# ScalarE's copy of a weight slot in two halves, each with its own signal to GpSimd

## Time and profile before

| | us |
|---|---|
| median of 3 runs | 2040.75 |
| lowest and highest | 2040.41, 2041.22 |
| the profiled execution's own time | 2041.43 |
| its span, first to last instruction | 2039.6 |
| TensorE busy | 1947.3 |
| VectorE busy | 1171.2 |
| GpSimd busy | 996.3 |
| ScalarE busy | 746.4 |

### The profile page before, as it was taken

How to read it: one execution, slowest core, us unless ns; L and a number is a source line. 1 busy time by engine, 2 the same in 40 slices (tenths; PEclk the granted TensorE clock), 3 DMA queues, 4 the chain that set the end, 5 groups by cost and what they waited for, 6 DMA issues and landing times.

```text
span 2039.6 us, 24806 instructions
## 1 busy us (share of the span) xinstructions
PE 1947.3 (95%) x9028; PEld 1609.5 (79%) x9028; DVE 1171.2 (57%) x2101; ACT 746.4 (37%) x1096; POOL 996.3 (49%) x1271
## 2 busy tenths in 40 slices
PE   7999989999899899999999999998999999999997
PEld 5778768787778778788888888787887888888886
DVE  6996659977676657655332324666576553232335
ACT  5334434335324445333322313344454223232230
POOL 5334253342543344656646456633344656464643
PEclk9999999999999999999999999999999999999998
DMA  4221122221222222222322222221122222222221
GB/s 173 89 75 67 56 83 104 76 73 63 73 83 71 75 83 76 90 103 83 109 93 94 103 98 88 86 101 62 63 83 104 94 92 99 87 104 103 83 103 63
DMA packets 28058, 178.92 MB, mean 88 GB/s; under 512 B 3872, under 2 KB 4000, under 8 KB 7456
## 3 DMA queue, kind: packets, MB, share of 16 engines
q1 hardware_dynamic: 24192, 169.88, 23.5%
q10 hardware_dynamic: 3744, 7.45, 1.1%
HBM read 175.22 MB, written 2.10 MB: 87 GB/s over the span
## 4 chain that ended last, share of the span: by engine, by line
PE 70%; DVE 18%; issue 6%; ACT 4%; POOL 2%; ACTq 0%; DVEq 0%
PE bank L533 63%; PE bank L554 3%; DVE bank L1796 3%; POOL W_lo L505 2%; DVE PR L1718 1%; PE bank L581 1%; PE bank L593 1%; DVE PR L1739 1%; DVE PT_lo L1592 1%; ACT PR L1171 1%; PE bank L572 1%; DVE Y_lo L1592 1%; ACT W_hi L1137 1%; ACT PT_hi L1141 1%; ACT Y_hi L1141 1%
## 5 line engine op out<-in xcount | busy, mean ns | idle before, releaser
L505 POOL TENSOR_TENSOR W_lo<-W_raw,W_hi 128x256 fp32r<-128x256 f32 (+1 forms) x1228 | 972.3, 830 | 995.1 <-ACT W_hi L1137 995.1
L533 PE MATMUL bank<-H_hi,W_hi 128*128 128x512 f32 x1264 | 503.5, 398 | 8.9 <-POOL W_lo L505 5.1
L533 PE MATMUL bank<-H_hi,W_lo 128*128 128x512 f32 x1264 | 495.2, 392 | 0.0
L533 PE MATMUL bank<-H_lo,W_hi 128*128 128x512 f32 x1264 | 494.7, 391 | 0.0
L533 PE MATMUL bank<-Y_hi,W_hi 128*128 128x512 f32 x972 | 386.2, 397 | 14.0 <-POOL W_lo L505 9.7
L533 PE MATMUL bank<-Y_lo,W_hi 128*128 128x512 f32 x972 | 382.0, 393 | 0.0
L533 PE MATMUL bank<-Y_hi,W_lo 128*128 128x512 f32 x972 | 382.0, 393 | 0.0
L1137 ACT ACTIVATE W_hi<-W_raw 128x2048 fp32r<-128x2048 f32 (+2 forms) x159 | 295.9, 1861 | 195.1 <-DMA W_raw<-in_stream 194.7
L533 PEld LDWEIGHTS bank<-H_hi,W_hi 128*128 128x128 f32 x1264 | 239.6, 190 | 59.7 <-POOL W_lo L505 5.5
L533 PEld LDWEIGHTS bank<-H_hi,W_lo 128*128 128x128 f32 x1264 | 238.9, 189 | 51.4
L533 PEld LDWEIGHTS bank<-H_lo,W_hi 128*128 128x128 f32 x1264 | 239.7, 190 | 47.6
(11 more groups left out here) (300 smaller groups left out, 2326.4 us busy)
## 6 DMA issues: line engine op xcount, KB each, us to landing
W_raw<-in_stream SPq DMA_DIRECT2D x160, 1024.0 KB, 4.8
BT<-in_bias ACTq DMA_DIRECT2D x8, 320.0 KB, 3.0
X<-in_x ACTq DMA_DIRECT2D x4, 512.0 KB, 7.2
out<-X SPq DMA_DIRECT2D x8, 256.0 KB, 2.2
BT<-in_rope ACTq DMA_DIRECT2D x2, 512.0 KB, 3.7
MC<-in_causal ACTq DMA_DIRECT2D x2, 256.0 KB, 3.3
MS<-in_window ACTq DMA_DIRECT2D x1, 321.0 KB, 8.2
NM<-in_columns ACTq DMA_DIRECT2D x1, 320.0 KB, 10.0
```

What stands on the lines that cost most here:

```text
L505: ins = nc.gpsimd.tensor_tensor(W[1][:, s, part], W_raw[:, s, part], W[0][:, s, part].bitcast(F32), ALU.subtract)
L533: mm = pe.matmul(out, lhs[a], rhs[b], start=(not begun and k == 0 and a == 0 and b == 0), stop=(not more and k == n - 1 and a == 1), skip_ ...
```

## The change

ScalarE makes the copy of every unit in two ACTIVATEs: the first four slices, then the rest. Each raises `w_hi` by one, so unit n has the values 2n + 1 and 2n + 2. Between them ScalarE waits for the instruction before the first of the two. GpSimd waits for the first value before slice 0 and for the second before slice 4; the slices in between carry no wait of their own. In the first three units the same two waits stand before slices 0 and 4, where every slice had one. The semaphore `w_half` is gone: the very first unit's copies, which were two already, now raise `w_hi` to 1 and 2. A unit of 1280 columns is split into 1024 and 256, the one of 768 into four and two half slices of 128 columns.

```diff
@@ low_part
-            pool.wait_ge(w_hi, n + 1)
             for k, part in enumerate(used(n)):
+                if k in (0, KT // 2):
+                    pool.wait_ge(w_hi, 2 * n + (1 if k == 0 else 2))
                 ins = nc.gpsimd.tensor_tensor(W[1][:, s, part], W_raw[:, s, part],
                                               W[0][:, s, part].bitcast(F32), ALU.subtract)
@@ first three units
         for n in range(EARLY):
             for kt in range(KT):
-                if n == 0 and kt < KT // 2:
-                    pool.wait_ge(w_half, 1)
-                else:
-                    pool.wait_ge(w_hi, n + 1)
+                if kt in (0, KT // 2):
+                    pool.wait_ge(w_hi, 2 * n + (1 if kt == 0 else 2))
@@ prep
             parts = used(n)
-            if parts[0].stop == P:
-                ends = [t[:, n % SLOTS, :].rearrange("p (k n) -> p k n", n=256)[:, 0:len(parts), 0:P] for t in (W[0], W_raw)]
-            else:
-                ends = [t[:, n % SLOTS, 0:parts[-1].stop] for t in (W[0], W_raw)]
-            nc.scalar.activation(ends[0], ends[1], ACT.Copy).then_inc(w_hi, own.reach(w_hi, n + 1))
+            for half in range(2):
+                first, last = (0, KT // 2) if half == 0 else (KT // 2, len(parts))
+                if parts[0].stop == P:
+                    ends = [t[:, n % SLOTS, :].rearrange("p (k n) -> p k n", n=256)[:, first:last, 0:P]
+                            for t in (W[0], W_raw)]
+                else:
+                    ends = [t[:, n % SLOTS, parts[first].start:parts[last - 1].stop] for t in (W[0], W_raw)]
+                if half:
+                    act.wait_ge(*own.last(1))
+                nc.scalar.activation(ends[0], ends[1], ACT.Copy).then_inc(w_hi, own.reach(w_hi, 2 * n + 1 + half))
@@ ScalarE's start
-        for part, signal in ((slice(0, 1024), (w_half, 1)), (slice(1024, 2048), (w_hi, 1))):
+        for part, signal in ((slice(0, 1024), (w_hi, 1)), (slice(1024, 2048), (w_hi, 2))):
```

More of the change, by code:

```diff
@@ L216, in _build @@
     w_lo = sem("w_lo")
-    w_half, w_tiles = sem("w_half"), sem("w_tiles")
+    w_tiles = sem("w_tiles")
     squared = sem("squared")
```

## The result

| | before | after |
|---|---|---|
| median of 7 runs, us | 2041.0 | 2046.9 |
| lowest and highest | 2040.41, 2042.82 | 2043.86, 2049.19 |
| profiled execution's own time, span | 2041.43, 2039.6 | 2047.72, 2045.9 |

The changed kernel is slower: ratio 1.0027, 95% interval 1.0015 to 1.0038, which is 3.1 to 7.8 us. The forecast was 2038.4 us with a range up to 2043.8; the measured time lies above that range. It lies within 0.3 us of the price that rival 2 ("collisions win") gave, which is partly luck, as the last bullet on the prediction shows.

The account below looks back on a forecast made before the run. TensorE was taken as the bound, 70% of the chain, with VectorE saturated in one stretch. Terms -3.84 - 1.0 + 1.4 + 1.7 - 1.4 + 0.8 = -2.3 us gave 2038.4 on the median, range 2034.2 to 2043.8.

Parts of the forecast that it names:

- rival 2: Softmax steps of both blocks: GpSimd's batches start ahead of VectorE's scalings, so slower, +5.9 us, 2046.6; chance 0.10.
- Start of GpSimd, the four stalls: Where matmuls wait for slices: GpSimd starts 0.86 us earlier, four stalls give 3.44, two other places 0.4; -3.84 us.
- Clock behind the stalls: Behind the four stalls: TensorE's lower clock may end earlier or not come; -1.0 us, bounds -5 and +3.
- rival 1: At the stalls: they take the lower clock with them and collisions cancel; -5.8 us, about 2034.9; chance 0.27.
- ScalarE's second copy: All units: 0.10 us more per pair, counting at 15 places on the chain; +1.4 us, bounds 0 and 15.
- VectorE in the first block: Softmax scalings there: GpSimd's earlier slices delay some and free others; +1.7 us, bounds -1.8 and +4.9.
- the four counted pairs: L1739 scalings at 104 and 122 us, both first-block layers: each pair ends 0.7 us later, 2.8 in all.
- The place behind 223 us: First block, a pair of scalings in each layer: only the second instruction is caught, 0.35 us, twice, 0.7.
- the four L1726: First block, two-column scalings at 203.95 and 230.83 us, both layers: now behind the batch's end, 4 x 0.45 = 1.8 back.
- VectorE in the heads: Second block's heads: batches end earlier, some scalings gain and others wait; -1.4 us, bounds -5.4 and +4.
- The three instructions that I followed: Second block's heads: L1739 at 645.93 2.2 us back, L1726 at 644.44 waits 1.8, L1726 at 735.31 1.0 back.
- Sums: Pool mixer's sums, about four chain places: two-input work overlapped by earlier slices, 0.2 us each; +0.8, bounds 0 and 2.

Follow-up runs that it names:

- Stalls only: Changed kernel with two copies and early start only in units before which matmuls wait for slices and the first three, one copy elsewhere: 2032.95 us, ratio 0.9958.

## Why the prediction was wrong

- **Start of GpSimd, the four stalls (-3.84): right.** Waits for slices 11.2 us (forecast 11), the long stall 4.1 (forecast 4.2), copies 14.6 us more in all (forecast 15). The places near 1264 and 1287 gave 1.0 us (forecast 0.4).
- **Clock behind the stalls (-1.0): right in kind, too small.** Stalls only gained 8.6 us where 4.8 was forecast for stalls and clock together, of it some 0.5 us at the start of the program. In its trace the clock gave back 4.6 us behind the four stalls and took 1.6 at 568 us, so -3.0. The forecast of rival 1 that the clock goes with the stall was the right half of it.
- **ScalarE's second copy (+1.4): not contradicted**, 0 to +3.7 with the early start taken away.
- **VectorE in the first block (+1.7): failed.** Alone these units cost 6.7 us (4.3 to 9.2), above the bound of 4.9. By the starts in the trace of that kernel the four counted pairs cost 3.2 us (forecast 2.8). The place behind 223 us costs 1.1 in each layer (forecast 0.35), since L1990, with two SBUF inputs, is hit as well. The forecast 1.8 came back at the four L1726, but 0.9 of it was lost again at once, where VectorE then waited for ScalarE. So the counted places cost 4.5 us. Uncounted were L1804, 0.3 us in each of four places, and the pair of L1970 and L1973, 0.85 us in each layer, of which 0.55 comes back at L1883: 1.9 us together, and the rest is small. I had looked at one-input scalings and left out two-input work that comes to stand beside slices. The pair behind 141 us was taken as covered: it lost 0.9 us and had 0.7 back 6 us later. (Line numbers here and below are those of the kernel before.)
- **VectorE in the heads (-1.4): the step that failed most.** Alone +4.1 to +9.2 us, above its bound of +4. The three instructions that I followed behaved nearly as said, and gave some 1.0 us back. The places that I did not follow decided it. By the starts in the trace of that kernel, L2251 costs 0.4 us in two places of each layer (0.69 to 1.08), and the first of them brings TensorE's lower clock behind it, 1.4 us more, in both layers. L1701 costs 0.4 to 0.9 us a layer and L2189 some 0.3. The diagonals at 574 cost nothing, as shown above. The term was a selection of examples and was summed as if it were a census.
- **Sums (+0.8): too small for the same reason.** In the same trace VectorE falls behind by 1.3 us at the sums of the pool mixer in each layer (an L2211 grew from 0.69 to 1.11 us) and has 0.6 back behind them, so +1.4.
- **Rival 2** had the mechanism and the place, and the price nearly by luck. Its collisions (8.3) and ScalarE's copy (1.4) make 9.7 us where the two parts measured 13.2, and its stalls give 3.84 where they gave 8.6: two errors that cancel. I gave it 0.10 because batches also end earlier. That gives back less than it takes: at an early start the first slice meets work that was free of slices, and what gets free at the end of a batch is in part lost again to the next wait.

## What to carry to other kernels

Starting a helper engine earlier is not free for an engine that it can block: list every instruction of the other engine in the time that the helper newly covers and in the time that it leaves, over the whole span, and sum both. Make the earlier start only where something waits for its result; here it was worth 8.6 us in ten units and cost 13 in sixty-two others. An instruction that grows costs time only where nothing covers it, so follow each one to the next wait. Where the helper must run beside short work, smaller instructions helped in this kernel, but only together with the earlier start, since the batch gets longer.

## What the hardware showed unexpectedly

A GpSimd instruction of 128 columns takes 0.51 us on average and one of 256 columns 0.84, in the same run: half slices cost 22% more of GpSimd's time. A VectorE operation with two SBUF inputs also pays (0.69 to 1.10 us and over), while the one with an accumulator in PSUM does not (L1796 takes 0.76 us with and without slices). And in the kernel before one VectorE instruction waited not for one slice but for the whole of the run: in its timeline

```profile
831.98 5.64 DVE L2392 TENSOR_TENSOR TMP<-TMP 128x512 f32<-128x512 f32 x1
...
819.46 17.62 POOL L505 TENSOR_TENSOR W_lo<-W_raw,W_hi 128x256 fp32r<-128x256 f32 x24 [13.24 <-ACT W_hi L1137]
```

the operation that takes 0.69 us at the median ended 0.5 us after 24 slices in a row had ended. It is 2 of the 16 instances, the first one of each layer. It sits beside a stretch that matmuls fill and cost nothing there; why it could not slip in between two slices, as others do, stays open.
